# Fifty column blocks of an input projection made ahead in pairs by seven products, kept in DRAM and loaded back

## What is computed

```
D_MODEL = 2048; SEQ = 512; HEAD_DIM = 128; D_FF = 5632
h = rms_norm(x, attn_norm_g[layer])
(q_n, kc_n, vc_n, ks_n, vs_n, kw_n, vw_n, g_n,
 q_f, k_f, v_f, f_l, m_a, m_b) = jnp.split(h @ w_in[layer], offsets, axis=-1)
y_nsa = nsa_attention(q_n, kc_n.., vc_n.., ks_n.., vs_n.., kw_n.., vw_n.., g_n, ...)
y_fox = fox_attention(q_f, k_f, v_f, f_l, fox_forget_bias[layer])
merged = (jax.nn.sigmoid(m_a) * (y_nsa @ w_branch_nsa[layer])
          + jax.nn.sigmoid(m_b) * (y_fox @ w_branch_fox[layer]))
x = x + merged @ w_out[layer]
h = rms_norm(x, ffn_norm_g[layer])
u, v = jnp.split(h @ w_up[layer], 2, axis=-1)
x = x + (jax.nn.gelu(causal_dwconv(u)) * v) @ w_down[layer]
```

## Time and profile before

| | |
|---|---|
| device time, median of 3 runs | 2707.33 us (2707.0 to 2708.76) |
| span of the profiled execution | 2706.5 us |
| PE busy | 2682.0 us, 99% |
| DVE busy | 1693.2 us, 63% |
| ACT busy | 1105.2 us, 41% |
| POOL busy | 430.9 us, 16% |
| DMA, mean over the span | 165 GB/s |

### The profile page before, as it was taken

How to read it: one execution, slowest core, us unless ns; L and a number is a source line. 1 busy time by engine, 2 the same in 40 slices (tenths; PEclk the granted TensorE clock), 3 DMA queues, 4 the chain that set the end, 5 groups by cost and what they waited for, 6 DMA issues and landing times.

```text
span 2706.5 us, 37208 instructions
## 1 busy us (share of the span) xinstructions
PE 2682.0 (99%) x13921; PEld 2279.0 (84%) x13921; DVE 1693.2 (63%) x2152; ACT 1105.2 (41%) x1396; POOL 430.9 (16%) x336
## 2 busy tenths in 40 slices
PE   8999999999999999999999999999999999999998
PEld 6888888888888888888888999999999998888886
DVE  4445552333333333342279999999999998888876
ACT  5334442222223232232255555555555544444445
POOL 0003333332344233300000000000000000000002
PEclk9999999999999999999999999999999999999999
DMA  6432228999588769983434353444434446566654
GB/s 181 119 109 59 74 78 237 256 252 236 165 210 220 194 186 248 251 212 127 155 109 129 108 136 105 127 117 109 135 105 127 117 112 234 212 224 224 227 204 154
DMA packets 473106, 445.39 MB, mean 165 GB/s; under 512 B 9093, under 2 KB 370198, under 8 KB 472233
## 3 DMA queue, kind: packets, MB, share of 16 engines
q1 hardware_dynamic: 431095, 327.29, 40.3%
q0 software_dynamic: 36112, 106.36, 16.2%
q10 hardware_dynamic: 5826, 10.76, 1.2%
HBM read 403.44 MB, written 105.94 MB: 188 GB/s over the span
## 4 chain that ended last, share of the span: by engine, by line
PE 93%; DVE 2%; issue 2%; ACT 2%; DMA 1%; POOL 0%; SPq 0%; DVEq 0%; ACTq 0%; POOLq 0%
PE bank L637 15%; PE bank L639 15%; PE bank L638 15%; PE bank L1006 14%; PE bank L1119 14%; PE bank L1016 9%; PE bank L1008 7%; PE bank L829 2%; PE bank L823 1%; DMA d_raw<-in_w_down_dram 1%; DMA w_raw<-in_w_in_dram 0%; ACT l_win L1235 0%; ACT l_slc L1235 0%; DVE ring_lo L1918 0%; PE bank L879 0%
## 5 line engine op out<-in xcount | busy, mean ns | idle before, releaser
L637 PE MATMUL bank<-hl,w_hi 128*128 128x512 f32 x1248 | 494.6, 396 | 2.4 <-DVE w_lo L1610 2.4
L639 PE MATMUL bank<-hl,w_lo 128*128 128x512 f32 x1248 | 487.3, 390 | 0.0
L638 PE MATMUL bank<-hl,w_hi 128*128 128x512 f32 x1248 | 487.0, 390 | 0.0
L1600 DVE TENSOR_TENSOR w_lo<-w_raw,w_hi 128x2048 fp32r<-128x2048 f32 x107 | 246.0, 2300 | 267.2 <-ACT w_hi L1137 266.9
L1137 ACT ACTIVATE w_hi<-w_raw 128x2048 fp32r<-128x2048 f32 x107 | 204.6, 1913 | 435.4 <-PE bank L639 401.7
L1006 PE MATMUL bank<-hl,ring_hi 128*128 128x512 f32 x1032 | 368.4, 398 | 0.5 <-ACT v_sb L1412 0.5
L1119 PE MATMUL bank<-fold_hi,y_slot 128*128 128x512 f32 x1120 | 344.8, 389 | 0.0
L1008 PE MATMUL bank<-hl,ring_lo 128*128 128x256 f32 x1032 | 289.8, 281 | 0.0
L639 PEld LDWEIGHTS bank<-hl,w_lo 128*128 128x128 f32 x1248 | 234.8, 188 | 49.6
L637 PEld LDWEIGHTS bank<-hl,w_hi 128*128 128x128 f32 x1248 | 235.1, 188 | 48.7 <-issue 3.0
L638 PEld LDWEIGHTS bank<-hl,w_hi 128*128 128x128 f32 x1248 | 235.1, 188 | 45.8
(11 more groups left out here) (323 smaller groups left out, 5006.9 us busy)
## 6 DMA issues: line engine op xcount, KB each, us to landing
w_raw<-in_w_in_dram SPq DMA_DIRECT2D x76, 1024.0 KB, 7.2
raw<-in_w_up_dram SPq DMA_DIRECT2D x43, 1024.0 KB, 7.1
raw<-in_w_up_dram SPq DMA_DIRECT2D x86, 512.0 KB, 7.9
w_s<-in_w_down_dram POOLq DMA_DIRECT2D x30, 1024.0 KB, 12.9
x_raw<-in_w_down_dram SPq DMA_DIRECT2D x30, 1024.0 KB, 5.1
nb<-in_w_down_dram POOLq DMA_DIRECT2D x40, 512.0 KB, 4.7
w_n<-nb POOLq DMA_DIRECT2D x40, 512.0 KB, 6.1
x_raw<-w_s SPq DMA_DIRECT2D x20, 1024.0 KB, 5.5
```

The costliest lines, as they stand in the source:

```text
L637: mm(dst, l_hi, r_hi, start=first, stop=False)
L638: mm(dst, l_hi, r_lo, start=False, stop=False)
L639: return mm(dst, l_lo, r_hi, start=False, stop=final)
L1600: V.tensor_tensor(w_lo[:, s.par, :], w_raw[:, s.par, :], w_hi[:, s.par, :].bitcast(F32), ALU.subtract).then_inc(w_ready, 1)
```

## The change

**Which blocks.** Of the 76 blocks four (QN0 to QN3) are made in plain slots at the start. 50 (`PAIRED`: all KV, QN4 to QN7, all QF, KF, VF, MA0 to MA9) are made next, two at a time, in 25 units of seven products, by the scheme of the up projection (175 products, `qkv_period`; own rings `q_ring_hi`, `q_ring_lo`). POOL multiplies each result by the token's factor and SP stores it in `p_dram`. 22 (`PLAIN`: MA10 to MA15, MB0 to MB15) stay plain slots and stand as fillers: one ahead of the compression (`S_PRE`), one within it, one per NSA head, a cover slot, and one per FOX head.

**What follows from it.** For the scheme the second quarter of h (`y12`) is saved in DRAM, replaced by sums and restored after the products. At the start ACT copies each of the 16 k-tiles of h a second time, to `m32`. The KV blocks are loaded from `p_dram` (`kv_fm`, 3 MB), and so are q, k and v of each head. The compression slots follow each other. The merges have one slot per pair, the branch slot, and load two gate blocks (0.5 MB) per pair from `p_dram` into one of two `gate_t`. FOX heads have one filler slot. POOL's 40 negations are spread over the products (24) and the two merges (8 each), the sums in DRAM over heads, merges and W_out.

```diff
+START_BLOCKS = [("QN", 0), ("QN", 1), ("QN", 2), ("QN", 3)]
+PAIRED = ([("KV", j_) for j_ in range(12)] + [("QN", j_) for j_ in range(4, 8)] + [(n_, j_) for n_ in ("QF", "KF", "VF") for j_ in range(8)]
+          + [("MA", j_) for j_ in range(10)])
+QKV_UNITS = len(PAIRED) // 2 + 1
+QKV_PRODUCTS = 7 * (QKV_UNITS - 1)
+PLAIN = [("MA", j_) for j_ in range(10, 16)] + [("MB", j_) for j_ in range(16)]
...
 S_KV = 0
-S_KW = S_KV + 4
-S_QN = S_KW + 12
-S_GA = S_QN + 8
-S_FOX = S_GA + 24
-S_GB = S_FOX + 24
-S_WO = S_GB + 24
+S_PRE = 4
+S_QN = S_PRE + 6
+S_COVER = S_QN + 9
+S_BA = S_COVER + 1
+S_FOX = S_BA + 8
+S_BB = S_FOX + 10
+S_WO = S_BB + 8
 S_UP = S_WO + 16
+PRE_ORDER = [2, 3, 0, 1]
+QKV_QUARTERS, MERGE_QUARTERS = 24, 32
...
-    gate_t = at("gate_t", A_ + 32 * KB, [P, 2, SEQ])
+    gate_t = [at(f"gate_t{b}", A_ + (32 + 4 * b) * KB, [P, 2, SEQ]) for b in range(2)]
...
+        def store_qkv(r):
+            v, u = PAIRED[2 * r - 2:2 * r] if r else START_BLOCKS[2:4]
+            sp.wait_ge(qkv_ok, 2 * r + 1)
+            sp.dma_start(block_in(u), q_u[:, r % 2, :]).then_inc(qkv_put[r % 2], 16)
+            sp.wait_ge(qkv_ok, 2 * r + 2)
+            sp.dma_start(block_in(v), q_v[:, r % 2, :]).then_inc(qkv_put[r % 2], 16)
...
+        last = unit(QKV_UNITS - 1)
+        sp.wait_ge(piece_ok, last.q + 5)
+        load_block(slot(S_PRE), PLAIN[0])
...
+        load_w1(slot(S_PRE + 1), 0, 0)
+        store_qkv(QKV_UNITS - 2)
+        sp.wait_ge(prod_done, QKV_PRODUCTS - 2)
+        for z in range(2):
+            sp.dma_start(hl[:, z, 0:KH, TH:SEQ].bitcast(F32), y12_dram[z]).then_inc(start_put, 16)
+        sp.wait_ge(qkv_put[0], 16 * QKV_UNITS)
+        sp.wait_ge(qkv_put[1], 16 * QKV_UNITS - 32)
+        sp.wait_ge(prod_done, QKV_PRODUCTS)
+        kv_at = BLOCK_AT["KV", 0]
+        for part, (a, b) in enumerate(((0, 4), (4, 12))):
+            sp.dma_start(kv_fm[:, a:b, :], p_dram[kv_at + a:kv_at + b].rearrange("n p t -> p n t")).then_inc(kv_in[part], 16)
+        sp.dma_start(sel[:], c_sel).then_inc(kv_in[1], 16)
+        store_qkv(QKV_UNITS - 1)
...
+        load_w1(slot(S_PRE + 2), 0, 1)
+        load_block(slot(S_PRE + 3), PLAIN[1])
+        load_w1(slot(S_PRE + 4), 1, 0)
+        load_w1(slot(S_PRE + 5), 1, 1)
+        store_plain(0, o_pre[:, 0, :])
...
+            def load_gates(p):
+                sp.wait_ge(br_read[which], p + 1)
+                a = BLOCK_AT[name, 2 * p]
+                sp.dma_start(gate_t[p % 2][:], p_dram[a:a + 2].rearrange("n p t -> p n t")).then_inc(g_in[p % 2], 16)
+
+            for p in range(8):
+                if p:
+                    load(slot(base + p), wbr[which][:, :, 256 * p:256 * p + 256], n=256)
...
+                if p < 7:
+                    load_gates(p + 1)
...
+        for h in range(HEADS):
+            load_block(slot(S_FOX + 2 + h), PLAIN[14 + h])
+            if h < HEADS - 1:
+                load_bias_f(h + 1)
+                load_fox_qk(h + 1)
+                load_fox_v(h + 1)
+            else:
+                load(slot(S_BB), wbr[1][:, :, 0:256], n=256)
+            store_plain(12 + h, o_fox[:, h % 2, :])
...
+            qkv_narrow(now.q, b, y11, bank_a[par], True)
+            pe.wait_ge(c11_out, now.n)
+            if r == 1:
+                pe.wait_ge(c21_out, 1)
+            qkv_wide(now.q + 1, b + 1, y21, bank_b, True)
+            if r >= 2:
+                pe.wait_ge(c12_out, now.n - 1)
+            else:
+                pe.wait_ge(y_part, 1)
+            (qkv_wide if r < QKV_UNITS - 1 else qkv_narrow)(now.q + 2, b + 2, q_t1_, bank_c[par], True)
+            pe.wait_ge(p1_out, now.n + 1)
+            if r == 1:
+                pe.wait_ge(y_part, 2)
+            qkv_narrow(now.q + 3, b + 3, t2_, bank_a[par], False)
+            if r >= 2:
+                pe.wait_ge(c22_out, now.n)
+                pe.wait_ge(y_part, 4)
+                qkv_wide(now.q + 4, b + 4, t4_, bank_a[1 - par], False)
+                pe.wait_ge(p5_out, now.n)
+                qkv_wide(now.q + 5, b + 5, y22, bank_c[1 - par], False)
+            pe.wait_ge(u2_out, now.n + 1)
+            if r == 1:
...
+            A(m32[:, k, :], pb[4 + k % 4][:], ACT.Copy, scale=cols[:, G_ATTN + k:G_ATTN + k + 1]).then_inc(xm_done, 1)
...
+            for p in range(8):
+                act.wait_ge(g_in[p % 2], (4 * which + p // 2) * 16 + 16)
+                A(gate_t[p % 2][:], gate_t[p % 2][:], ACT.Sigmoid).then_inc(sig_done[which], 1)
+                hi(slot(base + p + 1))
+                if which and p in (2, 4, 6):
+                    merged_hi(p // 2 - 1)
...
+            for p in range(8):
+                lo(slot(base + p + 1))
+                if which and p in (2, 4, 6):
+                    merged_lo(p // 2 - 1)
+                dve.wait_ge(sig_done[which], p + 1)
+                dve.wait_ge(w_used, slot(base + p).n + 3)
+                for j in range(2):
+                    dst, got, gate = m32[:, 2 * p + j, :], pb[2 * (p % 2) + j], gate_t[p % 2][:, j, :]
+                    if which == 0:
+                        r = V.tensor_tensor(dst, got[:], gate, ALU.mult)
+                    else:
+                        link(V.tensor_tensor(gate, got[:], gate, ALU.mult))
+                        r = V.tensor_tensor(dst, dst, gate, ALU.add)
+                r.then_inc(br_read[which], 1)
...
+                G.tensor_tensor(d, d, (rbc_q if block[0] in ("QN", "QF") else rbc)[:], ALU.mult).then_inc(qkv_ok, 1)
```

More of the change, by code:

```diff
@@ L463, in _ @@
             if c < 2:
-                load_cols(slot(c), win, COL_KV + c * P)
+                load_block(slot(c), START_BLOCKS[c])
         for c in range(2, 4):
[L466 to L475, removed]
@@ L492, in _ @@
[L492 to L499, removed]
-                    load(slot(base + 3 * pair + 2, 6, i), wbr[which][:, :, ds(i * (4 * P) + 2 * pair * P, 2 * P)], n=2 * P)
-        load_merge(S_GA, COL_MA, 0)
@@ new lines, in _ @@
+        s = slot(S_PRE)
+        for n, part in enumerate(PRE_ORDER):
+            pe.wait_ge(*((part_ready, 2 * 3 + n + 1) if n < 3 else (w_ready, s.n + 3)))
+            if part == 0:
+                pe.wait_ge(start_put, 96)
+            for k in range(4 * part, 4 * part + 4):
+                w = slice(k * P, k * P + P)
+                last = three(pb[0][:], w_hi[:, s.par, w], w_lo[:, s.par, w], h_hi[:, k, :], h_lo[:, k, :],
+                             n == 0 and k == 4 * part, n == 3 and k == 4 * part + 3)
@@ L1184, in _, with q_piece, q_piece_x @@
         A(fz[:, 1], fz[:, 1], ACT.Ln, bias=1.0).then_inc(fe_ok, 1)
-        hi(slot(3))
+        def q_piece(q, b, src):
+            if not isinstance(q, int) or q >= RING:
+                act.wait_ge(prod_done, q - (RING - 1))
+            A(q_ring_hi[(b + 3) % RING][:], src, ACT.Copy).then_inc(piece_hi, 1)
+        def q_piece_x(q, b, m, row, half):
+            if row == 0:
+                act.wait_ge(n0_in[m.r % 2], m.half * 16 + 16)
+            else:
+                act.wait_ge(n1_in[m.r % 2], m.half * 32 + 32)
+            q_piece(q, b, raw[m.r % 2][row][:, half, :])
@@ new lines, in _, with xs_high @@
+        qkv_period(1)
+        with act.Fori(0, (QKV_UNITS - 6) // 4) as i:
+            for r in range(2, 6):
+                qkv_period(r, i)
+        for r in range(QKV_UNITS - 4, QKV_UNITS):
+            qkv_period(r)
+        last = unit(QKV_UNITS - 1)
+        q_piece_x(QKV_PRODUCTS - 1, QKV_PRODUCTS - 1, last, 1, 1)
+        act.wait_ge(prod_done, QKV_PRODUCTS - 2)
+        hi_parts(slot(S_PRE), order=PRE_ORDER)
+        q_copy4(last, QKV_PRODUCTS)
+        def xs_high(kv):
+            for g in range(GROUPS):
+                A(xs_hi[:, :, g * CP:g * CP + CP], strides(kv, g), ACT.Copy)
+            A(xs_hi[:, :, 2 * CP:X_COLS], positions(kv), ACT.Copy).then_inc(xs_hi_ok, 1)
@@ L1328, in fox_step @@
             A(pt_f[:, 1024:1280], pb[5][:, 0:256], ACT.Copy).then_inc(ft_act, 1)
-            if fill > 1:
-                hi(slot(c + 2, per, i))
-                hi(slot(c + 3, per, i))
+            if more:
                 fox_hi(h + 1)
@@ L1851, in fox_lo, with fox_step @@
                 V.tensor_tensor(dst[:], src[:], high[:].bitcast(F32), ALU.subtract).then_inc(f_lo_ok, 1)
[L1854 to L1860 removed]
+        fox_lo(0)
+        lo(slot(S_FOX + 1))
+        plain_out(12, o_fox[:, 0, :], 0, slot(S_FOX))
+        def fox_step(h, b, use, done, fill, more):
             dve.wait_ge(bf_loaded[b], use * 16 + 16)
```

1108 lines of the change are left out of this document (696 added, 412 removed).

## The result

The changed kernel takes **2816.8 us** (median of 4 runs, 2808.0 to 2819.7), the kernel before 2707.5 (2707.0 to 2708.8): a ratio of 1.040 with a 95% interval of 1.038 to 1.041, so 109 us slower. Forecast were 2808 us and +101. The profiled span is 2817.7 us against 2706.5.

A forecast was written before the change was run, and what follows sets the result against it. PE was taken to bound the kernel (99% of the span, 93% of the chain). The terms −47 + 4 + 17 + 2 + 56 + 63 + 6 = +101 on 2707.3 gave 2808 us, range 2738 to 2860.

The forecast's parts named there:

- pairs and start: Products made in 25 two-block units save 1.88 us each, −47; extra k-tile copies and the first unit's split at the start, +4.
- junction: After the products, PE waits for the last store, then the first compression slot's high and low parts: +17 (8 to 25).
- NSA heads and cover: In the NSA heads, entry and cover slot wait once each for a store: +2 (0 to 5).
- merge A: Branch load queued behind the waiting gate load, so two buffers act as one; PE idles 8.0 us in seven cycles: +56.
- merge B: Same wait, with a longer multiplication: PE idles 8.3 us in seven cycles, plus two low parts of merged tiles: +63.
- FOX heads: Filler weights load behind PE's transposes of v, so exponentials and POOL's scaling come late in seven heads: +6 (0 to 26).
- third rival: Seven products run slower than in the up projection, 2 us more per unit, so the pairs gain nothing: 2858 us; chance 0.07.
- T0: The end of the last product; the last store after the products was put at 19 us behind it.
- first rival: In both merges POOL's sums don't meet the branch loads, which land in 7.2 us: +33, 2740 us; chance 0.18.
- fourth rival: In the merges PE's clock falls after each idle stretch, so pairs run slower: +25, 2833 us; chance 0.08.
- L = 15: Case of branch loads landing in 15 us in both merges; with 25 us after the products, 2854 us, inside the range.

The follow-up runs named there:

- the first experiment: The changed kernel, but in both merges SP issues the next pair's branch load ahead of its gate load, which waits for DVE: 2764.1 us.

## Why the prediction was right, and where it was off

| term of the sum | forecast, us | trace after, us |
|---|---|---|
| pairs and start | −47 + 4 | −42.7 + 1.3 |
| junction | +17 | +14 |
| NSA heads and cover | +2 | +1 |
| merge A | +56 | +50 |
| merge B | +63 | +56 |
| FOX heads | +6 | +29 |
| sum | +101 | +109 (the medians differ by 109, the spans by 111) |

**The pairs.** The narrow products of the chain stand at the same place of two periods at

```profile
200.91 2.88 PE bank L863 x24
...
220.79 2.88 PE bank L863 x24
```

19.88 us apart, as in the earlier trace rows to the hundredth. The first product starts at 83.08 us, where the fourth block's result was read at 81.8 before; the last ends at 584.4. That is 501.3 us for 50 blocks that took 544, with 2.2 us of waits in the first unit inside. The third rival (slower products) is out.

**The junction.** 11.3 us of idle and 0.06 of 48.7 us in lost clock (an estimate from the window) make 14. The chain is the one forecast (last store, high part, low part), but the store landed 15.3 us after T0 instead of 19, so PE's first wait was 8.3 us instead of 12.5; the other waits came to 3.0 where the sum had 2.7, and the lower clock to 2.9 where it had 2. In the 15.3 are about 2 us by which starting `sel` held the store up; the forecast didn't have them.

**The merges.** The mechanism was as written and the cycle 18.0 and 18.8 us where 18.9 and 19.2 were forecast, plus the merged low parts. In A the landing was 12.1 in the middle of seven, against 12.4, and the other parts of a cycle took 5.9 us instead of 6.5. In B they took 7.5 instead of 8.2, and the landing was 10.0 in the middle (10.7 on average), against 11. The extra low parts of the merged tiles (2.3 and 3.1 us) stood in cycles of 17.9 and 18.4 us, whose landings were short (8.1 and 7.6), so these cycles aren't the long ones; the longest is the first of each merge, 21.5 us. Seven cycles less 7 × 10.88 give 50 and 56. Not all of that is idle time: in merge A PE waits 36.0 us in seven stretches, 5.1 each instead of the 8 forecast, and the rest of each cycle is longer because its work runs at a lower clock. The first rival (short landings) failed on its condition: POOL's sums do meet the branch loads. The run without them shows what it would have been, 12.5 and 14.4 us a pair. The Trainium skill, "DMA: Bandwidth & Descriptors", section "Issuing engines are not separate DMA queues", says the same in general: transfers that different engines start run on the same DMA engines and interleave; the trace agrees, 6.5 us without POOL's transfers and 12.1 with them.

**The FOX heads** are the step that failed in size. The chain of causes is right (load behind the transposes of v, high part, exponentials, POOL's scaling, transposes), but the landing was taken from the heads before, 7.8 us; it was 11.2 in the middle of the seven loads that stand behind the transposes of v, and the stalled heads had up to 14.9 between issue and high part. The load of v, a store and the next bias load stand next to the weights in SP's queue, and POOL's 1 MB transfers run at the same time; how much each of them adds no run separates. There were four waits of 3.8 to 7.9 us instead of seven of 0.6, and about 8 us of lower clock behind them (an estimate, 0.06 of 139; the run with the weights a head earlier got back 25.7 us where idle time fell by 19.3, which leaves 6), which the term hadn't at all. The +29 is the window from 985 to 1145 us; the fourth wait, 3.8 us in the last head, lies behind it and is in no row of the table. In the merges the lower clock is hidden; in the heads, where PE sets the pace as soon as the wait ends, it isn't.

**The fourth rival**, the clock, was half right: pairs after an idle stretch did run lower, 0.88 and 0.85 on average, but a cycle of 18 us had room. With PE kept busy the median is only 3 us lower, less than either kernel's runs differ among themselves. That the sum came within 8 us is in part luck: 13 too much in the merges and 3 each at the junction and the start stand against 23 too little in the FOX heads and 4 in the pairs.

**Two slips in the working.** With L = 15 in both merges and the junction at 25 the sum is 2862 us, not 2854, and lies just outside the range. And the DMA digits from the ninth to the sixteenth slice run from 5 to 9, not from 7 to 9. Neither changes the forecast.

**What I did not see**: how much POOL's work is tied to the merges' length. The prediction held POOL to be a source of contention only; the first experiment showed that it is a stage of its own, 134 us per merge, hidden only while the merge is slow. Its waits are not in the sum, as they don't arise in the changed kernel.

## What to carry to other kernels

A load that waits only for its buffer is a prefetch; put it behind another load on the same queue that waits for late work, and the two buffers act as one, at the price of the whole landing per round. Before a stage is shortened, list what else runs under it (here POOL's 134 us) and find it another place, or the gain comes back as a wait behind the stage. And read an experiment's stage first and its total second: the first run's total fell into the rival's range, and in the stage that it changed theory 1 was right.

## What was not expected of the hardware

- The same 1 MB branch load took 6.5 us with POOL's transfers left out and 12.1 with them, at a DMA share of 0.93 in merge A. Moving the pairs closer together (10.9 instead of 18.0 us) left it at 12.4.
- A granted clock of 0.85 over 137 us cost nothing that could be measured where the stage's cycle was set by a load, and by estimate 6 to 8 us where PE followed at once (clock 0.94 over 160 us).
- 24 accumulating transfers of up to 1 MB each and 12 plain ones beside the up projection left the landing of its weights at 7.1 and 7.5 us (7.1 and 7.9 before) and its time unchanged.
- Starting a 33 KB load (`sel`) kept SP's queue busy for 3.85 us after the products, and for 1.68 us in the run with the stores first; a 1 MB load of weights took 0.4 to 0.8 us to start in merge A.
